# Two layers of a hybrid streaming encoder: the output projections of both attention stages done once, at the stage's end; residual adds on VectorE; norm matmuls at other places

## The reference

```python
# trunk, for each of the 2 layers
h = rms_norm(x, norm_g[i, 0])
o = gla_mixer(h, ...) if i % 2 == 0 else swa(h, ...)      # both end with  o @ w_out (+ b_out)
x = x + rms_norm(o, norm_g[i, 1])
h = rms_norm(x, norm_g[i, 2])
x = x + rms_norm(squared_relu_mlp(h, mlp_w_up[i], mlp_w_down[i]), norm_g[i, 3])

# rms_norm:      x * rsqrt(mean(x * x, -1) + 1e-6) * g
# squared_relu:  square(relu(h @ w_up)) @ w_down,  1024 -> 4096 -> 1024
# gla_mixer:     4 heads, keys of 128 and values of 256; per head a gated recurrence in chunks of 64 tokens;
#                o = rms_norm per head * g_onorm * silu(r);  return o @ w_out
# swa:           16 query heads of 64 on 4 key heads, each chunk of 64 sees itself and the 2 chunks before,
#                a sink logit joins each softmax;  return o @ w_out + b_out
```

## Time and profile before

| what | value |
|---|---|
| median of 3 runs | 2834.14 us (2831.01, 2834.14, 2843.71) |
| the profiled execution: its own time | 2830.92 us |
| its span, from the first to the last record | 2829.0 us |
| mean granted clock of TensorE | 0.962 |
| TensorE busy | 2596.7 us, 92% of the span |
| VectorE busy | 1218.8 us, 43% |
| ScalarE busy | 860.1 us, 30% |
| GpSimd busy | 541.6 us, 19% |

### The profile page before, as it was taken

How to read it: one execution, slowest core, us unless ns; L and a number is a source line. 1 busy time by engine, 2 the same in 40 slices (tenths; PEclk the granted TensorE clock), 3 DMA queues, 4 the chain that set the end, 5 groups by cost and what they waited for, 6 DMA issues and landing times.

```text
span 2829.0 us, 39614 instructions
## 1 busy us (share of the span) xinstructions
PE 2596.7 (92%) x15574; PEld 2477.6 (88%) x15574; DVE 1218.8 (43%) x3140; ACT 860.1 (30%) x1854; POOL 541.6 (19%) x271
## 2 busy tenths in 40 slices
PE   6889898986899999999997999998599999999997
PEld 5778787875899999999997888887499999999996
DVE  5564646568522222221257356567832222222226
ACT  4343433334311211121134455555422112211211
POOL 1011111113312212221224111100422122112212
PEclk9999999997999999999997999999699999999998
DMA  2000100013211111111113100001311111111113
GB/s 100 30 29 31 36 31 29 30 38 100 69 45 45 44 44 44 39 43 44 56 56 116 45 23 24 23 24 38 96 61 45 45 44 44 44 44 44 44 56 116
DMA packets 63086, 138.96 MB, mean 49 GB/s; under 512 B 8560, under 2 KB 39920, under 8 KB 62960
## 3 DMA queue, kind: packets, MB, share of 16 engines
q1 hardware_dynamic: 31680, 100.76, 10.8%
q10 hardware_dynamic: 31280, 36.52, 4.2%
HBM read 117.85 MB, written 19.40 MB: 49 GB/s over the span
## 4 chain that ended last, share of the span: by engine, by line
PE 78%; DVE 14%; ACT 4%; issue 3%; ACTq 1%; DMA 0%; POOL 0%; SPq 0%; DVEq 0%; POOLq 0%
PE banks L202 54%; PE banks L182 12%; PE banks L1724 3%; PE banks L1193 2%; DVE norm_acc_x L469 2%; DVE norm_acc L455 2%; PE banks L1173 1%; PE banks L1824 1%; DVE gla_att L2268 1%; DVE y L516 1%; DVE y L1474 1%; PE banks L1184 1%; DVE h_lo L528 1%; DVE swa_prob L1490 1%; PE banks L1859 1%
## 5 line engine op out<-in xcount | busy, mean ns | idle before, releaser
L159 POOL TENSOR_TENSOR w_lo<-w_raw,w_hi 128x1024 fp32r<-128x1024 f32 x180 | 447.7, 2490 | 1983.7 <-ACT w_hi L152 1983.7
L202 PE MATMUL banks<-h_hi,w_hi 128*128 128x384 f32 x1872 | 428.0, 337 | 9.8 <-POOL w_lo L159 7.5
L202 PE MATMUL banks<-h_lo,w_hi 128*128 128x384 f32 x1872 | 414.1, 329 | 0.0
L202 PE MATMUL banks<-h_hi,w_lo 128*128 128x384 f32 x1872 | 413.5, 329 | 0.0
L202 PEld LDWEIGHTS banks<-h_hi,w_hi 128*128 128x128 f32 x1872 | 317.9, 190 | 22.2 <-issue 17.4
L152 ACT CAST w_hi<-w_raw 128x1024 fp32r<-128x1024 f32 x180 | 186.7, 1045 | 454.9 <-DMA w_raw<-in_units 452.8
L202 PEld LDWEIGHTS banks<-h_lo,w_hi 128*128 128x128 f32 x1872 | 319.9, 190 | 0.0
L202 PEld LDWEIGHTS banks<-h_hi,w_lo 128*128 128x128 f32 x1872 | 319.0, 189 | 0.0
L898 DVE TENSOR_TENSOR y<-banks,y 128x768 f32<-128x768 f32 x192 | 130.0, 719 | 401.6 <-PE banks L202 400.0
L202 PE MATMUL banks<-mlp_a_hi,w_hi 128*128 128x384 f32 (+1 forms) x1344 | 296.6, 329 | 1.5 <-issue 1.3
L202 PE MATMUL banks<-mlp_a_lo,w_hi 128*128 128x384 f32 (+1 forms) x1344 | 295.1, 327 | 0.0
(11 more groups left out here) (187 smaller groups left out, 4053.2 us busy)
## 6 DMA issues: line engine op xcount, KB each, us to landing
w_raw<-in_units SPq DMA_DIRECT2D x180, 512.0 KB, 3.3
x_scratch<-y ACTq DMA_DIRECT2D x48, 192.0 KB, 1.9
norm_x<-x_scratch ACTq DMA_DIRECT2D x48, 192.0 KB, 2.7
x_scratch<-y ACTq DMA_DIRECT2D x24, 160.0 KB, 1.8
norm_x<-x_scratch ACTq DMA_DIRECT2D x24, 160.0 KB, 2.8
norm_x<-in_x ACTq DMA_DIRECT2D x16, 192.0 KB, 2.8
out_y<-y SPq DMA_DIRECT2D x16, 192.0 KB, 2.9
y<-in_x SPq DMA_DIRECT2D x8, 192.0 KB, 4.1
```

Of the source, the lines that this page charges most:

```text
L159: c.nc.gpsimd.tensor_tensor(c.w_lo[:, s], c.w_raw[:, s], c.w_hi[:, s].bitcast(F32), ALU.subtract).then_inc(self.ready, 1)
L202: mm = chip.nc.tensor.matmul(chip.banks[:, 3 * s + b, 0:WIDTH[b]], w, x[:, k, COLS[b]], start=(k == 0 and n == 0), stop=(k == n_k - 1 and ...
```

## The change

It does these things:
- **Output projections.** A new class `EndWave`, from which `Gla` and `Swa` inherit, does the projection over all 8 inputs k at the end of the stage, in two halves of output tiles (m = 0 to 3, then 4 to 7), each over the three blocks. The heads' gated outputs stay in `y`, their parts in `h_hi` and `h_lo`. The banks are taken into y by ScalarE (`take_end`; for SWA with the bias). The output tiles inside both loops, their adds and their last waves go. The units of `w_out` are cut by output tile m.
- **Early parts.** GLA's last head splits the six earlier k inside pairs 5 to 7 (`early_high`, `early_low`) and multiplies them for m = 0 to 3 of block 0 at slot 18 and among the turns; SWA's tiles 6 and 7 hold the splits (`split_at`) and the last tile the first parts (`fill_at`).
- **Loops.** r takes one k at a slot, the Silus come after pairs 2 and 7 (3 and 8 in later heads), weights are cast after pairs 0, 2, 4 and 6. SWA's queries lie at the chunks of `Q_AT`.
- **Borders.** All residual adds are VectorE's; GpSimd has only weights. In both attention stages the norm steps of the last wave lie in the second half, q = 0 to 7 for each block. The norm matmuls of blocks 1 and 2 are placed later in the last and the first wave.
- **Start.** SP issues the loads of x blocks 1 and 2, behind weights 0 and 1, and 2 and 3. ScalarE runs one Sqrt on a tile that VectorE has set, ahead of all else.

```diff
-GLA_UNITS, MLP_UNITS, SWA_UNITS = 8 * GH, 8 * FF_GROUPS, 2 * KVP + 2 * KVP * GROUP
+GLA_UNITS, MLP_UNITS, SWA_UNITS = 6 * GH + KT, 8 * FF_GROUPS, 2 * KVP + KVP * GROUP + KT
...
-    def tensor_in_last_wave(self, pe, b, m):
-        if b and m == 1:
-            self.sums(pe, b - 1)
-        if b and m == 3:
-            self.spread(pe, b - 1)
-        if (b, m) == (2, KT - 1) and self.middle:
+    def tensor_in_last_wave(self, pe, b, q):
+        if (b, q) == (1, 1):
+            self.sums(pe, 0)
+        if (b, q) == (1, 3):
+            self.spread(pe, 0)
+        if (b, q) == ((2, 1) if self.last else (2, 4)):
+            self.sums(pe, 1)
+        if (b, q) == ((2, 3) if self.last else (2, 7)):
+            self.spread(pe, 1)
+        if (b, q) == (2, 7) and self.middle:
             self.sums_x(pe, 0)
...
         if (b, j) == (0, 0):
             self.spread_x(pe, 0)
             self.sums(pe, 2)
-        if (b, j) == (0, 1):
+        if (b, j) == (0, 2):
             self.spread(pe, 2)
+        if (b, j) == (0, 3):
             self.sums_x(pe, 1)
-        if (b, j) == (0, 2):
+        if (b, j) == (1, 0):
             self.spread_x(pe, 1)
-        if (b, j) == (1, 2):
+        if (b, j) == (1, 3):
             self.sums_x(pe, 2)
-        if (b, j) == (1, 3):
+        if (b, j) == (2, 0):
             self.spread_x(pe, 2)
...
+    def add_x(self, dve, b, k):
+        self.x_landed(dve, b, k)
+        dve.wait_ge(self.s.scaled, self.per_norm(KT) + KT * b + k + 1)
+        y = self.chip.y[:, k, COLS[b]]
+        self.chip.nc.vector.tensor_tensor(y, y, self.s.x[:, k % self.X_SLOTS, 0:WIDTH[b]],
+                                          ALU.add).then_inc(self.s.x_new, 1)
...
         if s < KT:
             self.scale(dve, b, s)
+        if self.first:
+            if s >= 2:
+                self.low(dve, b, s - 2)
+            return
+        if 1 <= s <= KT:
+            self.add_x(dve, b, s - 1)
+        if self.middle and s >= 3:
+            self.low(dve, b, s - 3)
+        if self.middle and s >= 4:
+            self.add_squares_x(dve, b, s - 3)
...
     def gpsimd_with_units(self, pool, next_unit):
-        self.gpsimd_block(pool, 0, 0, KT)
...
+        for i in range(4):
+            self.chip.stream.low(pool, next_unit + i)
...
+class EndWave:
+    HALF = KT // 2
...
+    def tensor_end_wave(self, pe):
+        for n in range(JOB_BANKS, NB * KT):
+            half, b, m = n // (NB * self.HALF), n // self.HALF % NB, n % self.HALF + self.HALF * (n // (NB * self.HALF))
+            for k in range(KT):
+                mm = self.end_part(pe, b, m, k)
+                if half and k == KT // 2 - 1:
+                    self.after.tensor_in_last_wave(pe, b, 2 * (m - self.HALF))
+            mm.then_inc(self.end_full, 1)
...
+            if half:
+                self.after.tensor_in_last_wave(pe, b, 2 * (m - self.HALF) + 1)
+    def scalar_end_wave(self, act, next_unit):
...
+        for b in range(NB):
+            for m in range(self.HALF):
+                take(b, m)
+                if b == NB - 1 and m:
+                    ws.high(act, self.end_unit + self.HALF + m - 1)
+        for b in range(NB):
+            for q in range(KT):
+                if q % 2:
+                    take(b, self.HALF + q // 2)
+                act.wait_ge(self.end_added, self.end_index(b, q) + 1)
+                self.after.scalar_in_last_wave(act, b, q)
...
-    R_AT = ((0, 2, 4, 6, 9, 11, 13, 15), (0, 1, 2, 3, 5, 6, 7, 8))
-    SILU_AFTER = ((3, 8), (1, 3))
+    R_AT = ((0, 0, 0, 0, 0, 1, 2, 3, 5, 6, 7, 8, 9, 10, 11, 12), (0, 0, 1, 2, 3, 4, 5, 6, 8, 9, 10, 11, 12, 13, 14, 15))
+    SILU_AFTER = ((2, 7), (3, 8))
...
+            if (h, at) == (GH - 1, self.FIRST_FILL):
...
+                for k in range(self.EARLY):
+                    self.end_part(pe, 0, 0, k)
...
-            if self.out_slot(h, at) is not None:
-                output_tile(h, self.out_slot(h, at))
...
-                if p == 3 and h:
-                    ws.high(act, self.unit(h, 6))
-                if p == 5:
-                    ws.high(act, self.unit(h, 7) if h else self.unit(1, 0))
-                if p == 7 and h:
-                    ws.high(act, self.unit(h + 1, 0))
+                if p in (2, 4, 6):
+                    ws.high(act, self.unit(h + 1, p // 2 - 1))
+                if h == GH - 1 and 5 <= p < 8:
+                    early_high(2 * p - 10)
+                    early_high(2 * p - 9)
...
+        act.wait_ge(chip.norm.warm, 1)
+        nc.scalar.activation(chip.rs_x[:], chip.rs_x[:], ACT.Sqrt)
...
-                if k == 3:
-                    before.load_first_x(act, 1)
-        before.load_first_x(act, 2)
...
-                chip.stream.load_first(sp)
+                for s in range(2):
+                    chip.stream.load_first(sp, s)
+                borders[0].load_first_x(sp, 1)
+                for s in range(2, SLOTS):
+                    chip.stream.load_first(sp, s)
+                borders[0].load_first_x(sp, 2)
```

More of the change, by code:

```diff
@@ L403, in high @@
             return
-        act.wait_ge(self.s.x_new, KT * (NB * self.added + b) + k + 1)
+        self.x_added(act, b, k)
+        if self.last:
+            if after < NB * KT:
+                self.load_x(act, after // KT, after % KT)
+            return
         nc.scalar.activation(self.chip.h_hi[:, k, COLS[b]], y, ACT.Copy,
@@ L427, in scalar_before_last_wave, with scalar_in_last_wave @@
             self.load_x(act, 0, k)
[L429 to L440, removed]
+    def scalar_in_last_wave(self, act, b, q):
+        self.square(act, b, q)
+        if (b, q) == (1, 2):
+            self.root(act, 0)
+        if (b, q) == ((2, 2) if self.last else (2, 6)):
+            self.root(act, 1)
+        if b == 1 and q >= 5:
+            self.high(act, 0, q - 5)
+        if self.last:
+            if b == 2 and q < 3:
+                for k in ((3, 4), (5,), (6, 7))[q]:
+                    self.high(act, 0, k)
+            if b == 2 and q >= 4:
+                self.high(act, 1, q - 4)
+        elif b == 2 and q < 5:
+            self.high(act, 0, q + 3)
     def add_squares(self, dve, b, m):
@@ new lines, in vector_in_last_wave @@
+    def vector_in_last_wave(self, dve, b, q):
+        if q:
+            self.add_squares(dve, b, q - 1)
+        elif b:
+            self.add_squares(dve, b - 1, KT - 1)
+        if (b, q) == (1, 2):
+            self.inverse(dve, 0)
+        if b == 1 and q >= 3:
+            self.step(dve, 0, q - 3)
+        if self.last:
+            if (b, q) == (2, 0):
+                self.steps(dve, 0, 5, 7)
+            if (b, q) == (2, 1):
+                self.step(dve, 0, 7)
+            if (b, q) == (2, 2):
+                self.step(dve, 0, 8)
+                self.inverse(dve, 1)
+            if b == 2 and q >= 3:
+                self.step(dve, 1, q - 3)
+        else:
+            if b == 2 and q < 6:
+                self.step(dve, 0, q + 5)
+            if (b, q) == (2, 6):
+                self.inverse(dve, 1)
+            if (b, q) == (2, 7):
+                self.step(dve, 1, 0)
@@ L934, in gpsimd @@
             ws.low(pool, u0 + 8 * (FF_GROUPS - 1) + i)
-        if self.after.last:
-            self.after.gpsimd_all_odd(pool)
-class Swa:
+class Swa(EndWave):
     SCALE = float(CHUNK) ** -0.5
@@ L1402, in scalar @@
                 if (t, c) == (last, 9):
-                    end_high(0)
-                if (t, c) == (last, 14):
-                    end_high(1)
-                if t == last and c >= 14:
-                    for b, m in self.end_jobs(c - 1):
-                        in_end_wave(b, m)
+                    last_high(0)
+                if (t, c) == (last, 15):
+                    last_high(1)
         copy_turned(last, NCH - 2)
@@ L1653, in unit @@
     def unit(self, h, j):
[L1655 removed]
+        return 6 * h + j
     def proj_of(self, h, n):
@@ L2351, in vector @@
             if j:
-                low_parts(GH, j - 1)
-        low_parts(GH, NB - 1)
-        for b in range(NB):
-            for m in range(KT):
-                n = KT * b + m
-                dve.wait_ge(self.end_full, n + 1)
-                y = chip.y[:, m, COLS[b]]
-                nc.vector.tensor_tensor(y, chip.banks[:, n % JOB_BANKS, 0:WIDTH[b]], y, ALU.add).then_inc(self.end_added, 1)
-                self.after.vector_in_last_wave(dve, b, m)
+                low_parts(j - 1)
+        low_parts(NB - 1)
+        self.vector_end_wave(dve)
     def gpsimd(self, pool):
```

591 lines of the change are left out of this document (221 added, 370 removed).

## The result

The changed kernel takes **2791.52 us**, the median of four runs (2785.36 to 2791.79), against 2834.66 (2831.01 to 2843.71): a ratio of 0.9838, 95% interval 0.9811 to 0.9865. That is 43 us less. The forecast was 72 less, 2762. The result lies inside the range, on its upper side, between the forecast and the rival in which the borders stay VectorE's.

What follows compares the result with a forecast made beforehand. TensorE was taken to lead the attention loops and VectorE the borders. From the profiled 2830.9 us, -6 + 9 - 38 + 18 - 19 - 30 - 5 = -71 gave 2760, with half the median's offset 2762; range 2717 to 2815.

Steps and rivals of the forecast that it cites:

- the rival in which the borders stay VectorE's: Borders: adds join VectorE's queue, subtractions block fully, matmuls behind waits run slow; 15 us each, 2807 to 2820; chance 0.22.
- start, to head 0's first projection: Start: loads issued by SP and the root's table loaded ahead of the data; -6 us (0 to -9).
- head 0, from there to head 1's scores 0: First attention stage, head 0: more projection steps ahead, both Silus and two more weights in the loop; +9 us (0 to +12).
- heads 1 and 2: First attention stage: 24 us of filler matmuls less per head; -19 us each, -38 (0 to -23 each).
- head 3 to the end of MLP 0's first wave: First attention stage's end: early splits, projection in two halves, then a first wave of 64; +18 us (+8 to +33).
- MLP 0 to the second attention stage: MLP 0's border, last wave's start to first wave's end: 135.8 us becomes 116.5; -19 (-30 to 0).
- second attention stage: Tiles lose filler matmuls, tiles 1 to 5 8 us each, while the end grows by 29; -30 us (+5 to -45).
- tail: Run's end: GpSimd's adds go, a root comes earlier, VectorE gets 12 adds more; -5 us (-8 to +3).
- a border's first wave: First wave behind a stage: TensorE's matmuls, norm matmuls and waits of 8 and 3; 64 us, 67 in MLP 0's border.
- The adds for nothing: Borders: 24 adds on VectorE cost 11 us and give back up to 11 in sums of squares.
- the rival that loops don't shorten: Attention loops: a chain over three engines sets the period, removed filler leaves holes; 2859 us, chance 0.10.
- The signs that I named for the end waves: End waves: TensorE over 90% busy in their second half if right; waits on weights or takes, costed at nothing, if wrong.

Runs made afterwards that it cites:

- the unread matmuls: The changed kernel with matmuls whose result nobody reads placed in TensorE's waits ahead of norm matmuls in the three middle borders: 2778.55 us.

## Why the prediction was right or wrong

| step | forecast | by the traces |
|---|---|---|
| start, to head 0's first projection | -6 | -4.8 |
| head 0, from there to head 1's scores 0 | +9 | +12.4 |
| heads 1 and 2 | -38 | -34.2 |
| head 3 to the end of MLP 0's first wave | +18 | +35.7 |
| MLP 0 to the second attention stage | -19 | -11.5 |
| second attention stage | -30 | -34.7 |
| tail | -5 | -2.0 |
| sum | -71 | -39.1 |

**The term that was mis-sized is a border's first wave**, 64, 67 and 64 in the forecast. From the end of the last wave's last matmul it took 75.0, 73.7 and 75.4. That is 29 of the 32 us missed; the rest cancels. I priced it by TensorE's account: 47.5 of matmuls, 6 of norm matmuls, waits of 8 and 3. The sum of the waits came near, 12.2 in GLA's border, but by luck: block 2's diagonal, for which I had 8, cost 3.7, and 5.6 went to block 1's, which I had not listed. The slow matmuls behind the waits, which only the rival counted, are not in the sum.

Two parts can be told apart. The first is VectorE's way to block 2's diagonal. I gave it 22 us from the end of the last wave, and a lag of 3 more in MLP 0's border; it took 28.6, 30.3 and 28.6. Operations stretched beside GpSimd's subtractions hold 4.1, 6.5 and 4.7 of that. The forecast allows 1.2 for each of four subtractions, and none of the terms that make up the 22 contains it. In another 3.9, 1.7 and 3.2 VectorE stood idle. The run with more VectorE work shows that this way sets the length, and the unread matmuls show that a faster TensorE doesn't shorten it. The second part is what follows: 46.4, 43.4 and 46.8 us, where the forecast leaves 42. It holds matmuls at 1.2 GHz, and there the unread matmuls gave back 1.9, 3.1 and 2.9. The Silu's wait is a third miss of this kind, told below under the loops; in the sum it hides behind a loop priced too high.

**The rival that the borders stay VectorE's** had the mechanism, and 15 a border for it; 10 was measured. Its terms one by one: blocked time 5, measured 2.7 in the mean without the subtractions; slow matmuls 6, measured 2.3 in the borders with most of them gone; the adds 4, of the wrong sign, since they gain 3. These don't add up to the 10, so the runs show who leads and not the whole bill: no run took VectorE's own steps away without giving them to another engine. The Trainium skill ("SBUF — State Buffer", Who interferes with whom) has a VectorE operation with two SBUF inputs and a GpSimd operation that reads SBUF exclude each other for a whole instruction. The rows agree: 2.62 us instead of 0.48 beside a subtraction of 2.98. By that rule four subtractions would cost 10 a border. In the traces only operations that start beside a subtraction pay, and in the changed kernel two did in full in the first border, four in the second. The Trainium skill's advice to take work off a full VectorE ("Perfetto Trace Analysis", Optimizing Scalar/DVE Operations) goes the other way than the run with the adds on GpSimd. Its doubt about moving work between these two engines is the part that held.

**The adds for nothing** held as a bound: 72 adds at 0.47 are 34 us, and in the sums of squares alone 36 x 0.535 = 19 came back. That GpSimd's trip would go as well was right, and was not in the sum.

**The loops.** Head 1 was forecast at 68 from scores 0 to 8 and took 70.6; the rival that loops don't shorten fell. But the 68 was met by luck, with a wait inside that I had not seen: 7.8 us a head for the Silu. Without it the head takes 61.9, so the rest of the loop was priced 6 too high, and no term of the forecast holds this wait: I listed the new slots and not what the first projection behind the Silu waits for. Tiles were forecast at -9.6 and came at 34.6 us a tile, -12.7: a filler was worth its matmuls, 1.5 us, and not the 1.2 that I took from tile 0, which has a different first third. The end behind the tiles cost 13 more than forecast, of which the first wave is 11. The signs that I named for the end waves held: TensorE was busy all of 79.4 us there, and no wait on its weights or its takes showed.

**Start.** The root came 6 us earlier and 4.8 were left at head 0's first projection. **Tail.** 2 instead of 5: behind the last spread the chain runs through a load of x, which I had hidden behind three other slots (3.19 us of the chain in the kernel before, 3.96 now), so fewer or faster adds shorten little there. In the kernel before, too, it was not a GpSimd add that came last: such an add, 0.87 us of the chain, released the load, and an add on VectorE followed it. The load now:

```profile
2783.06 3.96 DMA norm_x<-x_scratch
```

## What to carry to other kernels

Where two engines hand a chain of small operations back and forth, price the stretch by each engine's queue up to the hand-over, and take the longer: busy shares over the whole stretch didn't tell here which leads, one added operation per step did. Work taken out of a loop uncovers the waits that it lay beside, so look for what each remaining filler waits for, and move that first: here two slots were worth 26 us, set against the 43 of the whole change. Undo a change stage by stage even when it gains, since one part may pay for another.

## What the runs showed of the hardware

A GpSimd subtraction of 128x1024 stretched a VectorE addition of 128x320 from 0.48 to 2.62 us. VectorE scalings that read PSUM and start beside such a subtraction stayed at 0.60 to 0.62, as here between 709 and 715 us of the changed kernel:

```profile
709.58 4.98 POOL L158 TENSOR_TENSOR w_lo<-w_raw,w_hi 128x1024 fp32r<-128x1024 f32 x2 [1.67 <-ACT w_hi L151]
```

```profile
711.11 0.62 DVE L524 SCALAR_TENSOR_TENSOR y<-y,gains,banks 128x384 f32<-128x384 f32 x1 [1.34 <-PE banks L323]
```

The same residual add is 1.17 us on GpSimd and 0.58 on VectorE. That TensorE's granted clock could be raised from 0.86 to 0.95 through a stretch with 12 us of waits, and that the three borders gain only 7.0 us by it, all of it behind block 2's spread, I had not expected.
